# Third weight slot at the norm boundaries, squares added through a PSUM bank, and two jobs of the second recurrent head ahead of the first head's scores

## What is computed

```python
for layer in range(DEPTH_2):
    a = rms_norm(h, norm_gains[layer, 0])
    m = mla_mixer(a, ...) if layer % N_MIXERS == 0 else hgrn2_mixer(a, lower_bounds[layer], ...)
    h = h + rms_norm(m, norm_gains[layer, 1])
    a = rms_norm(h, norm_gains[layer, 2])
    h = h + rms_norm(sq_relu_mlp(a, mlp_w1[layer], mlp_w2[layer]), norm_gains[layer, 3])

def rms_norm(x, g):
    y = x * lax.rsqrt(jnp.mean(x * x, axis=-1, keepdims=True) + EPS)
    return y * g

def hgrn2_mixer(h, lb, ...):       # C = 32 tokens, 16 chunks
    q_x, f_x, i_x, g_x = jnp.split(h @ w_in, 4)
    f = lb + (1.0 - lb) * sigmoid(f_x);  k = 1.0 - f;  b = cumsum(log(f))    # per chunk
    a = where(causal, (q * exp(b - b_ref)) @ (exp(b_ref - b) * k), 0)
    o = a @ v + (q * exp(b)) @ state
    state = exp(b_last) * state + (k * exp(b_last - b)) @ v
```

## Time and profile before

| | |
|---|---|
| median of 3 executions (lowest, highest) | 1909.19 us (1907.77, 1910.06) |
| profiled execution, its span | 1907.2 us, 1905.2 us |
| mean granted clock of PE | 0.945 |
| PE busy | 1700.1 us (89%), 10588 matmuls |
| DVE busy | 870.4 us (46%) |
| ACT busy | 716.2 us (38%) |
| POOL busy | 636.7 us (33%) |
| load of 512 KB of weights, issue to landing | 4.0 us |
| HBM | 73 GB/s over the span |

### The profile page before, as it was taken

One profiled execution on the slowest core, in us unless ns is written; L12 is line 12 of the kernel. 1 busy time (PEld: TensorE's weight loads), 2 busy tenths in 40 slices (PEclk: granted clock), 3 DMA queues, 4 the chain that ended last, 5 costly groups with the idle time before them and its releaser, 6 DMA issues.

```text
span 1905.2 us, 29877 instructions
## 1 busy us (share of the span) xinstructions
PE 1700.1 (89%) x10588; PEld 1373.1 (72%) x10588; DVE 870.4 (46%) x1467; ACT 716.2 (38%) x1129; POOL 636.7 (33%) x385
## 2 busy tenths in 40 slices
PE   4999868778678999899999998699997899999997
PEld 4777737756455676887888887578786787888885
DVE  4644476655566543552212125666665443212125
ACT  1332333322343443452323234566564351323232
POOL 4344400003331112453444445223231544444441
PEclk8999969998788999899999998799999999999998
DMA  9423200001111112223333332122221323333331
GB/s 319 126 85 91 71 7 3 3 2 58 44 39 30 35 36 67 78 78 88 100 88 99 98 93 63 40 66 72 66 66 42 90 68 89 96 91 99 100 93 63
DMA packets 250852, 140.08 MB, mean 74 GB/s; under 512 B 10089, under 2 KB 242624, under 8 KB 250768
## 3 DMA queue, kind: packets, MB, share of 16 engines
q1 hardware_dynamic: 249072, 135.03, 24.2%
q10 hardware_dynamic: 688, 2.23, 0.3%
q0 software_dynamic: 1008, 1.66, 0.3%
HBM read 136.80 MB, written 2.10 MB: 73 GB/s over the span
## 4 chain that ended last, share of the span: by engine, by line
issue 42%; PE 33%; POOL 10%; DVE 9%; DVEq 4%; ACT 1%; POOLq 1%; ACTq 0%
PE bank L659 24%; POOL w_low L505 9%; PE bank L803 2%; PE bank L914 2%; DVE bank L1740 1%; DVEq L1747 1%; DVEq L2110 1%; DVE sum_sq L1740 1%; DVE sum_sq L359 1%; DVE mix_out L1740 1%; PE bank L817 1%; PE bank L1016 1%; POOL param_rows L486 0%; DVE kk_norm L1740 0%; DVEq L2045 0%
## 5 line engine op out<-in xcount | busy, mean ns | idle before, releaser
L505 POOL TENSOR_TENSOR w_low<-w_raw,w_high 128x1024 fp32r<-128x1024 f32 (+1 forms) x236 | 523.2, 2217 | 1144.8 <-ACT w_high L1271 1144.8
L659 PE MATMUL bank<-act_high,w_high 128*128 128x512 f32 x1000 | 399.0, 399 | 16.4 <-POOL w_low L505 14.2
L659 PE MATMUL bank<-act_high,w_low 128*128 128x512 f32 x1000 | 391.3, 391 | 0.0
L659 PE MATMUL bank<-act_low,w_high 128*128 128x512 f32 x1000 | 391.1, 391 | 0.0
L1271 ACT ACTIVATE w_high<-w_raw 128x1024 fp32r<-128x1024 f32 (+1 forms) x236 | 229.4, 973 | 297.7 <-PE bank L659 276.2
L659 PEld LDWEIGHTS bank<-act_high,w_high 128*128 128x128 f32 x1000 | 188.4, 188 | 64.8 <-issue 10.2
L659 PEld LDWEIGHTS bank<-act_high,w_low 128*128 128x128 f32 x1000 | 188.4, 188 | 41.0
L659 PEld LDWEIGHTS bank<-act_low,w_high 128*128 128x128 f32 x1000 | 188.6, 189 | 39.6 <-issue 2.0
L659 PE MATMUL bank<-hid_high,w_high 128*128 128x512 f32 x488 | 191.9, 393 | 4.5 <-DVE mix_out L2303 3.8
L659 PE MATMUL bank<-hid_high,w_low 128*128 128x512 f32 x488 | 191.3, 392 | 0.0
L659 PE MATMUL bank<-hid_low,w_high 128*128 128x512 f32 x488 | 191.2, 392 | 0.0
(11 more groups left out here) (486 smaller groups left out, 2888.0 us busy)
## 6 DMA issues: line engine op xcount, KB each, us to landing
w_raw<-in_mlp_w SPq DMA_DIRECT2D x128, 512.0 KB, 4.0
w_raw<-in_hgrn_w_in SPq DMA_DIRECT2D x32, 512.0 KB, 4.0
w_raw<-in_w_in SPq DMA_DIRECT2D x29, 512.0 KB, 4.0
w_ada_piece<-in_w_ada SPq DMA_DIRECT2D x6, 2048.0 KB, 13.7
w_raw<-in_w_out SPq DMA_DIRECT2D x8, 512.0 KB, 3.8
w_raw<-in_mla_w_o SPq DMA_DIRECT2D x8, 512.0 KB, 3.8
w_raw<-in_hgrn_w_o SPq DMA_DIRECT2D x8, 512.0 KB, 3.8
w_raw<-in_mla_w_in SPq DMA_DIRECT2D x6, 512.0 KB, 4.0
```

The source lines that it names most:

```text
L505: gp.tensor_tensor(WL[:, c0 % 2, 0:kt, 0:m], WR[:, c0 % 2, 0:kt, 0:m], WH[:, c0 % 2, 0:kt, 0:m].bitcast(F32), ALU.subtract).then_inc(w_lo, 1)
L659: mm = pe.matmul(PB[s][0:m, :], w[:, s, k, 0:m], a[:, k0 + k, :], start=(k == 0 and w is WH and a is hi), stop=(k == kt - 1 and w is WL))
```

## The change

1. A third extra slot Z. c0+6 gets X, c0+7 gets Z, c0+8 Y, and c0+9 and c0+10 the ordinary slots. ACT fills slots for c0+6 to c0+9 each before a square that stood before it, and POOL makes all low parts up to c0+10 ahead of `low_half(b, 0)`. At boundary 1 POOL's making of masks, which stands between `low_mlp` and `boundary`, thereby comes ahead of low(c0+6).
2. The squares of tiles 5 and 6 go to PSUM bank 5 instead of TMP. `token_stat` is divided: `token_sum` sums SQA inside 7h0 (for half 0) and 7h1 (for half 1), `token_stat` only adds the last square, in 5h1 and in job c0+8. DVE gives the signal `hf_sum` for half 1 behind the residual of half 0 and the add of tile 6. The two halves of bank 4 carry what `residual` kept in banks 4 and 5.
3. ACT makes high(G0+4) before the deviation of the norm ahead of HGRN, and high(G0+5) at HGRN's start. PE runs jobs G0+4 (bank 4) and G0+5 and transposes the values of head 0 before the scores of head 0; the iteration for head 1 then has two jobs only. DVE scales all four tiles of head 0 first. The norm sum's hook in after_head moves from behind k = 1 to behind k = 3.
4. The Exp of the lower bounds (ACT) moves from before MLP 0 into it, the eight small operations on them (DVE, `forget_bounds`) from before the norm ahead of HGRN into MLP 0.

The diff, cut to its core:

```diff
@@ -269,11 +271,14 @@
 
         def weights(c, c0):
 
-            if c == c0 + KT - 1 or c == c0 + KT + 3:
+            if c == c0 + KT - 2 or c == c0 + KT + 3:
                 return WHX, WLX
+            if c == c0 + KT - 1:
+                return WHZ, WLZ
             if c == c0 + KT:
                 return WHY, WLY
-            return WH[:, c % 2], WL[:, c % 2]
+            s = (c + 1) % 2 if c in (c0 + KT + 1, c0 + KT + 2) else c % 2
+            return WH[:, s], WL[:, s]
...
             def boundary(b, c0):
 
-                low_x(c0 + KT - 1, c0)
-                low_x(c0 + KT, c0)
-                low_x(c0 + KT + 1, c0)
+                for c in range(c0 + KT - 2, c0 + KT + 3):
+                    low_x(c, c0)
                 low_half(b, 0)
-                low_x(c0 + KT + 2, c0)
                 low_half(b, 1)
                 low_x(c0 + KT + 3, c0)
 
...
                 return ((wh, lo),)
 
+            def token_sum(b, h):
+
+                pe.wait_ge(hf_sum, 2 * b + h + 1)
+                for t in range(h * HALF_T, (h + 1) * HALF_T):
+                    pe.matmul(PB[2][:, t:t + 1], SQA[:, t * P:(t + 1) * P], ONES[:, 0:1], start=(t % HALF_T == 0),
+                              stop=False)
+
             def token_stat(b, h, n_act):
 
-                pe.wait_ge(hf_sum, 2 * b + h + 1)
                 pe.wait_ge(nm_act, n_act)
                 for t in range(h * HALF_T, (h + 1) * HALF_T):
-                    ts = slice(t * P, (t + 1) * P)
-                    pe.matmul(PB[2][:, t:t + 1], SQA[:, ts], ONES[:, 0:1], start=True, stop=False)
-                    mm = pe.matmul(PB[2][:, t:t + 1], TMP[(n_act - 1) % 2][:, ts], ONES[:, 0:1], start=False, stop=True)
+                    mm = pe.matmul(PB[2][:, t:t + 1], TMP[(n_act - 1) % 2][:, t * P:(t + 1) * P], ONES[:, 0:1],
+                                   start=False, stop=(t % HALF_T == HALF_T - 1))
                 mm.then_inc(hf_stat, 1)
 
...
-                    half_job(c0 + k, c0, tail_bank(c0, k, 0), 0, hi, lo, all_passes, last=lo).then_inc(half_done, 1)
+                    half_job(c0 + k, c0, tail_bank(c0, k, 0), 0, hi, lo, all_passes, last=lo,
+                             hooks={6: lambda: token_sum(b, 0)} if k == KT - 1 else None).then_inc(half_done, 1)
                 for k in range(WHOLE, KT):
                     if k > WHOLE:
                         pe.wait_ge(fr, f0 + 3 + k - 1)
                     half_job(c0 + k, c0, tail_bank(c0, k, 1), 1, hi, lo, all_passes, last=lo,
-                             hooks={3: lambda: token_stat(b, 0, n_act)} if k == WHOLE else None)\
-                        .then_inc(job_done, 1)
+                             hooks={2: lambda: token_stat(b, 0, n_act)} if k == WHOLE else
+                             {6: lambda: token_sum(b, 1)} if k == KT - 1 else None).then_inc(job_done, 1)
                     if k == WHOLE:
                         token_spread(b, 0)
 
...
@@ -970,11 +976,10 @@
                     pe.wait_ge(w_lo, c1 + i + 1)
                     pe.wait_ge(fr, f0 + 10 + i)
                     half_job(c1 + i, c0, head_bank(c1, i), 0, AH, AL, hi_passes, first=ready(act_hi, 0),
-                             hooks={3: lambda: token_stat(b, 1, n_act + 3)} if i else None)
+                             hooks={4: lambda: token_spread(b, 1)} if i else
+                             {5: lambda: token_stat(b, 1, n_act + 3)})
                 for i in range(2):
                     half_job(c1 + i, c0, head_bank(c1, i), 0, AH, AL, lo_pass, first=ready(act_lo, 0), last=AL)
-                    if i == 0:
-                        token_spread(b, 1)
                 pe.wait_ge(w_lo, c1 + 3)
                 pe.wait_ge(fr, f0 + 13)
                 half_job(c1 + 2, c0, head_bank(c1, 2), 0, AH, AL, all_passes, last=AL)
@@ -996,7 +1001,7 @@
...
-            def hgrn(n, o):
-
+            def hgrn(n, o, second=False):
+
+                if second:
+                    pe.wait_ge(w_lo, G0 + 5)
+                    for k in range(KT):
+                        for w, a in ((WH, AH), (WH, AL), (WL, AH)):
+                            mm = pe.matmul(PB[4][:, :], w[:, G0 % 2, k, :], a[:, k, :],
+                                           start=(k == 0 and w is WH and a is AH), stop=(k == KT - 1 and w is WL))
+                    mm.then_inc(job_done, 1)
+                    job(G0 + 5, 0, free["g"], 6)
+                    turn_values(0, None)
                 if o is not None:
                     pe.wait_ge(g_ops, o + 1)
...
                 squares[0] += 1
                 outs[0] += 1
                 act.wait_ge(mx_out, outs[0])
-                act.wait_ge(nm_sq, squares[0])
-                act.activation(TMP[(squares[0] - 1) % 2][:, cols], M[:, k, cols], ACT.Square).then_inc(nm_act, 1)
+                act.wait_ge(nm_sq, squares[0] + (0 if bank is None else 1))
+                dst = TMP[(squares[0] - 1) % 2] if bank is None else bank
+                act.activation(dst[:, cols], M[:, k, cols], ACT.Square).then_inc(nm_act, 1)
 
...
                         high(c0 + 1 + k)
+                    if k == WHOLE - 1:
+                        high_x(c0 + KT - 2, c0)
                     square_out(k, whole)
-                high(c0 + KT - 2)
-                square_out(WHOLE, HALF[0])
                 high_x(c0 + KT - 1, c0)
-                square_out(WHOLE + 1, HALF[0])
+                square_out(WHOLE, HALF[0], PB[5])
                 if not last:
                     high_x(c0 + KT, c0)
+                square_out(WHOLE + 1, HALF[0], PB[5])
+                if not last:
+                    high_x(c0 + KT + 1, c0, done=c0 + WHOLE)
                 square_out(WHOLE + 2, HALF[0])
                 dev(0)
+                spread(0, 0, 2)
                 if not last:
-                    high_x(c0 + KT + 1, c0, done=c0 + KT - 2)
-                spread(0, 0, 4)
-                square_out(WHOLE, HALF[1])
-                if not last:
-                    high_x(c0 + KT + 2, c0, done=c0 + KT - 1)
+                    high_x(c0 + KT + 2, c0, done=c0 + WHOLE + 1)
+                spread(0, 2, 4)
+                square_out(WHOLE, HALF[1], PB[5])
                 spread(0, 4, KT)
-                square_out(WHOLE + 1, HALF[1])
+                square_out(WHOLE + 1, HALF[1], PB[5])
                 square_out(WHOLE + 2, HALF[1])
                 dev(1)
                 if last:
                     return
                 spread(1, 0, KT)
-                high_x(c0 + KT + 3, c0)
+                high_x(c0 + KT + 3, c0, done=c0 + KT - 1)
                 for k in range(KT):
                     act.wait_ge(act_lo, (USE[b] + 1) * KT + k + 1)
                     act.activation(M[:, k, :], XH[:, k, :], ACT.Square).then_inc(pre_sq, 1)
...
                 norms[0] += 1
+                if l == 0:
+                    act.wait_ge(lb_diff, 1)
+                    act.activation(LBS[:, HEADS:3 * HEADS], LBS[:, HEADS:3 * HEADS], ACT.Exp).then_inc(lb_exp, 1)
...
-            act.wait_ge(lb_diff, 1)
-            act.activation(LBS[:, HEADS:3 * HEADS], LBS[:, HEADS:3 * HEADS], ACT.Exp).then_inc(lb_exp, 1)
             mlp(0, F0)
+            high(G0 + 4)
             deviation(D)
...
-                    t = TMP[(squares[0] - 1) % 2]
+                    t = TMP[(squares[0] - 1) % 2] if bank is None else bank
                     if first:
                         dve.tensor_copy(SQA[:, cols], t[:, cols]).then_inc(nm_sq, 1)
                     else:
-                        tt(SQA[:, cols], SQA[:, cols], t[:, cols], ADD).then_inc(nm_sq, 1)
...
                 def residual(h, k0, k1):
                     for k in range(k0, k1 + 1):
                         if k < k1:
-                            tt(PB[4 + k % 2][:, 0:inner], M[:, k, HALF[h]], PB[3][:, HALF[h]], MUL)
+                            tt(PB[4][:, HALF[k % 2]], M[:, k, HALF[h]], PB[3][:, HALF[h]], MUL)
                         if k > k0:
-                            stt(XH[:, k - 1, HALF[h]], PB[4 + (k - 1) % 2][:, 0:inner], gain(layer, which, k - 1),
+                            stt(XH[:, k - 1, HALF[h]], PB[4][:, HALF[(k - 1) % 2]], gain(layer, which, k - 1),
                                 XH[:, k - 1, HALF[h]], MUL, ADD)
                         dve.drain()
...
                     evict(k, HALF[0], tail_bank(c0, k, 0))
-                    add_square(whole if k == WHOLE else HALF[0])
+                    if k == WHOLE:
+                        add_square(whole)
+                    if k < KT - 1:
+                        add_square(HALF[0], bank=PB[5])
+                    if k == KT - 2:
+                        dve.sem_inc(hf_sum, 1)
                 rstd(0)
                 residual(0, 0, 4)
                 dve.wait_ge(job_done, c0 + WHOLE + 1)
                 evict(WHOLE, HALF[1], tail_bank(c0, WHOLE, 1))
                 residual(0, 4, KT)
-                for k in range(WHOLE + 1, KT):
-                    dve.wait_ge(job_done, c0 + k + 1)
```

(11 more changed lines are left out.)

92 lines of the change are left out of this document (55 added, 37 removed).

## The result

| | before | after |
|---|---|---|
| median of 6 executions (lowest, highest) | 1908.38 us (1898.85, 1910.06) | 1892.47 us (1891.46, 1893.78) |
| profiled execution, span | 1907.2, 1905.2 | 1893.6, 1891.7 |
| mean granted clock | 0.945 | 0.947 |

What follows compares the result with a forecast made beforehand. TensorE, busy 89% of the span, was taken as the bound, idle mainly at four norm boundaries and HGRN's start. Terms summed to -7.2 us: 1907.2 to 1900.0, or 1902.0 us on the median, range 1895 to 1909.5.

Steps and rivals of the forecast that it cites:

- Boundary 0, third slot: Boundary 0: a slot of its own for c0+6 only moves the wait from 6h0 to 7h0; 0.
- Head: Behind boundary 0: PE waits some 5.8 us for the token sum, then half clock; after_head at 818.4, +0.3 us.
- Exp: Start of MLP 0: without table load and Exp ahead, PE resumes at 824.05; -1.7 us, with the head -1.4.
- Boundary 1: Boundary 1: POOL's masks lengthen 6h0's wait by 1.0 us, the later 1.82 goes; -0.8 us.
- The head's loss is covered: Boundary 1: the head's loss costs nothing, since PE waits there for the norm anyway.
- Start of HGRN: Ahead of head 0's scores: held adds +2.3, last product -2.1, two jobs and transposes in PE's idle time; -1.5 us.
- Second head: Iteration for head 1: two jobs fewer, latency-bound at 28.0 instead of 33.5 us, clock costs 1.5; -4.0 us.
- The middle of 0 and 2.9: Second head: half clock costs 2.9 us if it begins with G0+6, nothing if with the outputs; 1.5 taken.
- Boundaries 2 and 3: Boundary 2 as boundary 0, within slack, 0; boundary 3 loses more behind the sums than its wait gains, +0.5 us.
- Rival 1: Boundaries and HGRN: the token sum's wait costs the clock twice, a longer half-clock stretch; 1914.4 us, chance 0.09.
- Rival 2: Boundaries, HGRN and Exp: every wait named goes in full, 23.7 us won; 1885.5 us, chance 0.08.
- Rival 3: HGRN's start: half clock at G0+4 and through G0+6 gives back 5.5 us; 1907.5 us, chance 0.20.

Runs made afterwards that it cites:

- e10: The change with 40 matmuls that nobody reads ahead of the token sum's wait in 7h1; 1884.78 us, ratio 0.9879 to the kernel before.
- e3: The change with the token sum of half 1 moved back beside token_stat, behind six k of job c0+8; 1887.56 us, ratio 0.9882 to the kernel before.
- e4: The change with ACT's high(G0+4) behind the deviation of the norm ahead of HGRN; 1890.44 us, ratio 0.9910 to the kernel before.
- e6: The change with the norm sum's hook in after_head back behind k = 1; 1895.76 us, ratio 0.9928 to the kernel before.
- e7: The change with POOL's masks for HGRN made ahead of MLP 0's low parts, behind boundary 0; 1891.98 us, ratio 0.9918 to the kernel before.
- e8: The change with the edits of e3, e4 and e7 and high(G0+5) behind head 0's sigmoid; 1887.96 us, ratio 0.9897 to the kernel before.
- e2: The kernel before with only points 3 and 4 of the change (HGRN and the Exp); 1897.80 us, ratio 0.9936.
- e9: The change with the edits of e3, e4 and e7 together; 1884.88 us, ratio 0.9877 to the kernel before.
- e11: The change itself run once more, for the scatter of its stages; one execution, 1891.74 us.

## Why the prediction was wrong

The place of nearly every wait was right, and the sum came out at half: -7.2 against -14.5 from S to the end. The step that failed first is the price of the half clock behind the token sum. The prediction counted it for 28 of PE's own matmuls, all behind the sum, and put the chain of the norm that runs through PE's queue, from the reciprocal of half 1 to the residual and from the norm sum to the root, at zero. The runs showed that 2.8 us of the half clock passed inside the wait and that the chain won 1.9 and 0.9 us at the start of HGRN alone. Next comes the second head, where two pieces were mis-sized. Nearly all of it failed in the same direction.

**Boundary 0, third slot, forecast 0, measured about -1.0.** The step that failed is the 4.7 us from the end of a low to the next high on that slot. I read it from a slot that is loaded from in_mlp_w. The slot in question is loaded from in_mla_w_o, and there it was 773.14 - (766.89 + 2.40) = 3.85. That the tensor makes the difference is not shown: two such lags from in_mla_w_o were 3.87 and 3.85 in this trace, two from in_mlp_w 4.74 and 4.24. So 7h0 waited only 1.17 and began 1.0 earlier from S (776.70 less 0.98, where before had 776.74). The new slot's own effect was as costed: the wait went from 6h0 to 7h0.

**Head, forecast +0.3.** The sum's start was 0.9 earlier from S than forecast, which is the 1.0 of 7h0 carried on; the length of the wait was right. What failed is the split of the 21.95 behind it: I set the whole half-clock stretch of 6.55 us behind the sum, and part of it elapsed inside the wait. Measured 20.85. The Trainium skill ("TensorE: Matmul & The Clock Gate", Part 1) has the clock follow how busy PE has been; e10 agrees, since with the wait filled the clock stayed at 1.00 and it was 19.03.

**Exp, with the head forecast -1.4.** PE began MLP 0 3.65 us earlier from S and waited for nobody. ACT was not ready at the forecast 823.95 but, from S, before 821.8 (822.77 less 0.98), since its squares follow the residual of half 1, and that was earlier by the first missing term:

**Missing: from half 1's reciprocal to its residual.** The move of `token_spread(b, 1)` from between the low passes into c0+9 stands in the diff and was never priced, nor was the clock that the matmuls ahead of it would have. DVE's next work waits for it. From the reciprocal to the first product of the residual passed, at boundary 0, 4.05 us before (801.28 to 805.33) and 1.78 after (801.58 to 803.36); at boundary 1 3.71 and 1.79. Before ran at half clock there, after at full. e3 has the new place at half clock (0.50 from 800.71 to 804.33) and took 3.62. So 0.4 us of the 2.3 at boundary 0 is the place and the other 1.8 the clock; at boundary 1 e3 took 3.29, which gives 0.4 and 1.5. No trace has the old place at full clock. At boundary 1 it stands on the path, as the norm ahead of HGRN follows.

**Boundary 1, forecast -0.8.** The wait of 6h0 grew to 3.62 (forecast 3.1) and that of 7h0 went, as said: -0.3 from the waits. From the first down projection to spread 1 it was -1.5 in the first pair of traces; before has a second half-clock stretch in the tail (1154.5 to 1157.9) that after lacks, and no run separates the two. "The head's loss is covered" was right, but the head had no loss.

**Start of HGRN, forecast -1.5, measured -3.4.** Term by term from spread 1: held adds +1.95 (forecast +2.3; shown by e4), the spread -1.9 (missing), the root -0.94 (missing: PE's norm sum, 2.08 at half clock before and 1.13 after; why the half clock came later is not shown, the hook's place is not the reason by e6), the norm's reciprocal to the last product 17.66 to 16.75, -0.9 (forecast -2.1: the product gave its 2.1, but high(G0+5) with 1.06 now stands ahead of the sigmoid), and the transposes 1.76 to 0.08, -1.7 (as forecast). These make -3.5.

**Second head, forecast -4.0, measured -6.2.** The piece from scores to mask took 2.4 us, not 3.6, as the row I read it from ran at half clock; from `scaled(0)` to the first state it was 3.3, not 2.8; and the clock cost 0.4, not 1.5. The half clock did come:

```profile
1220.30:1231.00 10.70, 10.66 (x43) 9.85 (x43) 7.31 (x17) 6.35 (x9) 3.55 (x2) 0.52 0.35 100
```

Most of it fell on the outputs, which wait for DVE's states, and its end on job G0+6:

```profile
1227.24 0.77 PE L661 MATMUL bank<-act_high,w_high 128*128 128x512 f32 x1
...
1234.36 1.02 PE L1231 MATMUL bank<-hg_out_sq,ones 128*128 128x512 f32 x2
```

From that job's start to the square sum it was 7.12 us, against 6.74 before at full clock (1241.55 to 1248.29), of which PE waited 1.00: so about 0.4 was paid. That it was so little is partly luck. In e3, e4, e6, e7 and e8 the half clock lasted 13.7 or 17.1 us and head 2 took 52.6 to 52.9, where it was 51.8; in e7 the same piece took 8.30 (1225.76 to 1234.06). The middle of 0 and 2.9 that I took was not far off for such an execution. The states (6.07) and the 15.5 from them to the next scores were right.

**Boundaries 2 and 3, forecast 0 and +0.5.** Measured -1.5 and +1.9; e2 and e8 show that code that is the same there differs as much between kernels, so I can attribute neither. What speaks for the forecast's mechanism at boundary 3 is that the three traces with the late sum (e3, e8, e9) have 323.6 to 325.2, all below the seven with the change's (325.5 to 327.3).

**The rivals.** Rival 1 (the clock twice) was right that the bare wait costs clock, and the length from which it saw the gain cancelled did appear (10.2 us in e11), but before had as long a stretch, the part inside the wait is free, and in e11 a later stretch was missing in return. It is why the change gave 14.5 and not the 24 of e10. Rival 2 was nearer in size and wrong in its reason: the waits did not go in full. Rival 3 did not happen: no half clock lay on job G0+4 and G0+5, and G0+6 paid 0.4, not 5.4.

**Open.** What decides between a stretch of 6.8 and one of 10.2 us, and what head 2 takes with none. Which of the slot, the bank and the divided sum won what at the boundaries; they were not tried singly. B2 and B3 by code. And why in e3, at boundary 0, a wait of only 2.18 was followed by 6.85 us of half clock.

## What to carry to other kernels

When a change moves a small instruction of a chain (here one spread), or the half clock around it, read what is queued ahead of it on its engine before and after and at which clock; the row that waits for it shows the price at once. Here the clock was four fifths of it. A row taken as a duration must be read with its clock: three of my terms came from rows at half clock, or left the clock out. And a wait of some us inside dense matmuls may be worth filling with matmuls that nobody reads, if the engine would have been idle anyway; here that gave 7.7 us, about half of what the change gave.

## What the runs showed of the hardware

- The part of a half-clock stretch that falls into a wait costs PE nothing: of 6.8 us at boundary 0, 2.8 lay there.
- The same instructions had 6.8 us of half clock in one execution and 10.2 in another, and the whole, from S to the end, differed by 1.0 us.
- The half clock reaches other engines through PE's small matmuls: from DVE's reciprocal to its first product it was 3.62 us at 0.50 (e3) and 1.78 at 1.00 (after), from the same code.
- Even a tensor_scalar of 128x8 elements took 2.25 us beside a POOL weight job, where a reciprocal of that size just before took 0.20:

```profile
1191.69 2.42 POOL L520 TENSOR_TENSOR w_low_x<-w_raw,w_high_x 128x1024 fp32r<-128x1024 f32 x1
...
1191.89 2.25 DVE L2339 TENSOR_SCALAR hg_bounds<-hg_bounds 128x8 f32<-128x8 f32 x1
```

- Four loads of 512 KB took 3.87 and 3.85 us (in_mla_w_o), 4.74 and 4.24 us (in_mlp_w) from the release of their slot to their use.
